# Attention on one core: turned weights weighed four groups at a time, in place of two

## The reference

```
p_c = masked_softmax(q . k_cmp)          # compressed keys, 63 blocks
p_s = masked_softmax(q . k_sel)          # selected blocks: with 1024 tokens, all causal ones
p_w = masked_softmax(q . k_win)          # window of 512
out = gate0 * p_c @ v_cmp + gate1 * p_s @ v_sel + gate2 * p_w @ v_win
```

## Time and profile before

| | |
|---|---|
| time, median of 3 | 1775.0 us (1772.59 to 1776.08) |
| profiled execution | 1776.86 us, its span 1774.8 us |
| TensorE busy | 1667.9 us, 94% of the span |
| VectorE, ScalarE, GpSimd busy | 1134.2, 734.2, 290.0 us |
| granted TensorE clock over the span | 0.966 |
| attention: first turn to last weigh | 392.1 to 653.0 us |

### The profile page before, as it was taken

The page is one execution under the profiler, slowest core; times in us unless marked ns, Lnnn a source line. Parts: engine busy times, 40 slices in busy tenths (PEclk is TensorE's granted clock), DMA queues, the critical chain, the costliest instruction groups (busy, mean ns, idle before and its releaser), DMA issues. The chain is left out here.

```text
span 1774.8 us, 34718 instructions
## 1 busy us (share of the span) xinstructions
PE 1667.9 (94%) x13909; PEld 1534.6 (86%) x13909; DVE 1134.2 (64%) x1886; ACT 734.2 (41%) x1379; POOL 290.0 (16%) x380
## 2 busy tenths in 40 slices
PE   6999999989999979999977897999999989999997
PEld 5999999978888867888753896999999989999997
DVE  6463485238877765766677678878777766545531
ACT  6532332127655554444443433334333344333431
POOL 1000000013333233222121321121121120000000
PEclk8999999999999999999978999999999999999999
DMA  6641265357977326777675761344444487666641
GB/s 183 127 108 36 58 158 166 120 162 229 255 141 139 81 96 229 234 230 243 181 134 166 219 187 59 124 164 138 144 145 165 167 304 248 193 192 185 184 128 54
DMA packets 294030, 287.48 MB, mean 162 GB/s; under 512 B 62238, under 2 KB 248182, under 8 KB 291246
## 3 DMA queue, kind: packets, MB, share of 16 engines
q1 hardware_dynamic: 266398, 179.79, 36.0%
q0 software_dynamic: 25088, 100.94, 18.5%
q10 hardware_dynamic: 2384, 4.53, 1.0%
HBM read 215.36 MB, written 107.60 MB: 182 GB/s over the span
## 5 line engine op out<-in xcount | busy, mean ns | idle before, releaser
L59 PE MATMUL pm<-ops,slots 128*128 128x258 f32 x1792 | 510.1, 285 | 19.7 <-DVE ops L3671 14.7
L60 PE MATMUL pm<-ops,slots 128*128 128x258 f32 x1792 | 508.7, 284 | 0.0
L61 PE MATMUL pm<-ops,slots 128*128 128x258 f32 x1792 | 507.6, 283 | 0.0
L59 PEld LDWEIGHTS pm<-ops,slots 128*128 128x128 f32 x1792 | 339.6, 190 | 20.8 <-DVE ops L3671 15.4
L61 PEld LDWEIGHTS pm<-ops,slots 128*128 128x128 f32 x1792 | 342.1, 191 | 0.0
L60 PEld LDWEIGHTS pm<-ops,slots 128*128 128x128 f32 x1792 | 341.8, 191 | 0.0
L59 PE MATMUL pz<-hH,winH 128*128 128x344 f32 x600 | 199.7, 333 | 1.6 <-DVE hL L845 1.6
L61 PE MATMUL pz<-hH,winL 128*128 128x344 f32 x600 | 193.6, 323 | 0.0
L60 PE MATMUL pz<-hL,winH 128*128 128x344 f32 x600 | 193.5, 323 | 0.0
L3677 DVE TENSOR_TENSOR slots<-uact,slots 128x512 fp32r<-128x512 f32 x160 | 109.6, 699 | 78.8 <-ACT slots L3497 78.5
L3497 ACT ACTIVATE slots<-uact 128x512 fp32r<-128x512 f32 x160 | 99.0, 625 | 126.4 <-DMA uact<-downS_scratch 39.3
(11 more groups left out here) (682 smaller groups left out, 3311.0 us busy)
## 6 DMA issues: line engine op xcount, KB each, us to landing
hidD_scratch<-onat POOLq DMA_DIRECT2D x112, 258.0 KB, 3.0
downS_scratch<-in_w_down_dram POOLq DMA_DIRECT2D x12, 2048.0 KB, 15.7
hs<-hidD_scratch SPq DMA_DIRECT2D x38, 516.0 KB, 4.9
uact<-in_w_up_dram SPq DMA_DIRECT2D x64, 256.0 KB
uact<-downS_scratch SPq DMA_DIRECT2D x64, 256.0 KB, 3.0
raw<-in_w_in_dram SPq DMA_DIRECT2D x24, 512.0 KB, 3.7
uact<-in_w_down_dram SPq DMA_DIRECT2D x48, 256.0 KB, 4.1
wo<-hidD_scratch SPq DMA_DIRECT2D x18, 516.0 KB, 4.7
```

What stands on the lines that cost most here:

```text
L59: nc.tensor.matmul(out, wH, mH, start=start and k == 0, stop=False)
L60: nc.tensor.matmul(out, wH, mL, start=False, stop=False)
L61: last = nc.tensor.matmul(out, wL, mH, start=False, stop=stop and k == n - 1)
```

## The change

The ring of SBUF buffers for turned weights (`ptT`) grows from four to five (`NPT`), the fifth being a tile of its own, `turned_more`, and the order on TensorE becomes: once five turned groups wait, four are weighed (`BATCH`). `craw`, used only at the start of the stage, moves into space that was already set aside. The waits of the copies for their buffer follow the new ring. `pT` stays at two banks, and the placing of the steps does not change. The copy of a finished tile of pO comes one group later in ScalarE's queue.

```diff
+NPT, BATCH = 5, 4
...
-        sb("ahead_rest", [P, 8 * P])
+        ahead_rest = sb("ahead_rest", [P, 8 * P])
...
-        ptT = [free2[:, n * 4 * P:(n + 1) * 4 * P] for n in range(4)]
-        craw = sb("craw", [P, 2, P])
+        turned_more = sb("turned_more", [P, (NPT - 4) * 4 * P])
+        ptT = [free2[:, n * 4 * P:(n + 1) * 4 * P] for n in range(4)] + [turned_more[:, n * 4 * P:(n + 1) * 4 * P] for n in range(NPT - 4)]
+        craw = ahead_rest[:, 0:2 * P].rearrange("p (k c) -> p k c", k=2)
...
-                    bank, src = O[t % 2], ptT[n % 4]
+                    bank, src = O[t % 2], ptT[n % NPT]
...
-                    if len(behind) == 4:
-                        weigh(behind.pop(0))
-                        weigh(behind.pop(0))
+                    if len(behind) == NPT:
+                        for _ in range(BATCH):
+                            weigh(behind.pop(0))
...
-                    if n >= 4:
-                        act.wait_ge(pv_done, n - 3)
+                    if n >= NPT:
+                        act.wait_ge(pv_done, n - NPT + 1)
                     w = len(sched.groups[n][2]) * P
-                    nc.scalar.activation(ptT[n % 4][:, 0:w], PT[n % 2][:, 0:w], ACT.Copy).then_inc(copied_a, 1)
+                    nc.scalar.activation(ptT[n % NPT][:, 0:w], PT[n % 2][:, 0:w], ACT.Copy).then_inc(copied_a, 1)
...
-                    if n - 4 == sched.tile_end[out]:
+                    if out < len(TILE_ORDER) and n - NPT == sched.tile_end[out]:
...
-                    if n >= 4:
-                        dve.wait_ge(pv_done, n - 3)
+                    if n >= NPT:
+                        dve.wait_ge(pv_done, n - NPT + 1)
```

More of the change, by code:

```diff
@@ L1607, in copy_turned @@
                     dve.wait_ge(pt_done, n + 1)
-                    if n >= 4:
-                        dve.wait_ge(pv_done, n - 3)
+                    if n >= NPT:
+                        dve.wait_ge(pv_done, n - NPT + 1)
                     w = len(sched.groups[n][2]) * P
-                    nc.vector.tensor_copy(ptT[n % 4][:, 0:w], PT[n % 2][:, 0:w]).then_inc(copied_v, 1)
+                    nc.vector.tensor_copy(ptT[n % NPT][:, 0:w], PT[n % 2][:, 0:w]).then_inc(copied_v, 1)
                 def gather_rows():
```

## The result

The changed kernel takes 1791.89 us, the median of 5 runs (1788.63 to 1795.98), against 1775.0 us for the one before (now 5 runs, 1772.59 to 1780.2). The ratio is 1.0085, with a 95% interval of 1.0062 to 1.0108: 15 us more, between 11 and 19. It is taken over all runs and is not the quotient of the two medians, which lie 16.9 us apart. The forecast was 1790 us, 15 us more.

What follows compares the result with a forecast made beforehand. TensorE was taken to bound the attention. Between counts of +20 and +5 us, both net of the saving, +15 us was chosen by judgement, giving 1790 us as a median; range 1771 to 1800.

Steps and rivals of the forecast that it cites:

- What the change saves: TensorE's borders between 128- and 64-column matmuls in the attention: 75 visits become 38, saving 11 to 12 us.
- The batches worked through: 15 of 37 attention batches, followed through each engine's queue: sum +8.0 us, mean +0.53 us, net of the saving.
- T17: Attention batch where a turn waits for ScalarE's copy behind exponentials: 7.94 us becomes 8.81 us, losing 0.9 us.
- T125: Attention batch where a turn waits for VectorE's copy: 5.23 us becomes 6.11 us, losing 0.9 us.
- T49: Attention batch where a score waits for pS banks: 0.35 us wait, about the 0.3 us saved, so even.
- The first count: Net loss over the attention's 37 batches, extended from the 15 worked through: +20 us.
- the coarse one: Overruns of attention turns losing their cover, 26.5 us, less old stalls 9.6 and saving 11.8: +5 us.
- Where the waits stand: TensorE waits for copies of turned weights in 40 to 60 places, at T(4m+3) and T(4m+4) alone, 0.3 to 1.7 us each.
- The chain from S29 to T20: Attention, score to turn through ScalarE's exponentials and copy: stays 5.0 to 5.2 us without the weighs between.
- The rival that the borders win: In the attention, idle engines catch up during four weighs, only the saving stays: up to -12 us; faster 0.15.
- The rival of a starved VectorE that then binds: VectorE idles during the attention's four weighs, then binds: +5 us on the 20, 1800 us; chance 0.06.
- The fifth buffer: Extra SBUF buffer for turned weights in the attention: claimed hidden, costed at nothing; otherwise 2 us a batch.

Runs made afterwards that it cites:

- the run of one at a time: One group weighed at a time instead of two, in the kernel before with its four buffers: 1795.43 us, ratio 1.0112.
- the chain cut: Changed kernel with ScalarE's copies of turned weights queued ahead of exponentials and VectorE's ahead of scalings, from group 6 on: 1774.48 us, ratio 0.9997 against the kernel before.

## Why the prediction was right

- *What the change saves*, 37 visits at 0.3 us, 11 to 12 us: the rest fell by 12.4 us, 11.5 without the two groups weighed ahead of T5, and the run of one at a time gives 0.33 us a visit. T20 with its four weighs takes 438.62 - 436.17 = 2.45 us, where 2.46 had been put together from pieces.
- *The batches worked through.* T17 +0.87 us (0.9 forecast), T125 +0.82 (0.9), T49 +0.14 (0), by the starts of the turns in both traces. Of the other twelve, T113 came to -0.29 (-0.3), T121 -0.50 (-0.6), T93 +0.44 (0.4) and T85 +0.92 (0.7); the furthest off are T129, +0.41 for 0.8, and T21, +0.27 for 0.6. All 15 sum to 6.4 us, where 8.0 had been forecast.
- *Which count.* The first count gave +20 us over 37 batches, the coarse one +5, and +15 was chosen between by judgement; no sum gives it, so that the value came out this close is partly luck. The counted stretch shows +15.9. By the starts of the turns all 37 batches, T1 to T149, sum to +17.7 us, a mean of 0.48: 0.43 for the 15 and 0.51 for the other 22. So the 15 were a fair sample, and the first count ran high by 0.1 us for each batch worked. The coarse count had the stalls too small, 26.5 us against 38.5; 7.1 us of the difference of 12.0 are the bank waits that it left out.
- *Where the waits stand.* At T(4m+3) and T(4m+4), as forecast, though not quite alone: 17 and 20 held turns, and T14 and T86. 39 places is just under the 40 to 60 named. The chain from S29 to T20 is 5.03 us, where 5.0 to 5.2 had been forecast.
- *The rival that the borders win* fell because the stalls came to 38.5 us in all, where 21 us, the 9.6 of before and the 11.8 saved, was the point of balance. Its argument, that idle engines would catch up, is what the chain cut refutes: with the same TensorE order and the same work on each engine the loss goes away, and it goes only by moving the copies. Throughput was not what lacked. The rival of a starved VectorE that then binds falls with it: that VectorE is busy for 39.98 of the 50 us from 400 us on, less than the 43.62 of before, shows by itself only that it waits more, but the same work fits once the copies come earlier.
- *The fifth buffer was costed at nothing.* By itself, with two at a time, it costs 2 to 7 us. The reading is that it shifts which turns have a weigh just ahead of them, at the expense of ScalarE's; with four at a time one turn of each engine lacks the weigh in either phase, so it need not add to the 15 us; that is argued, not shown. Against the run with the same ring and two at a time, four at a time has 22.9 us more of stalls and 12.9 us less of rest, 10 us in all, and the ratios are some 10 us apart as well. A ring of four with four at a time was not run. The later copy of a finished tile, also put at nothing, holds one weigh: W6 starts 0.15 us after it ends, 0.2 us late.
- *Not settled.* In the profiled execution the span grew by 11.8 us, but the stage by 18: the part behind it was 6 us shorter. The traces of the other runs put that part between 1115.7 and 1119.9 us, and before at 1121.5 us, so it varies; the medians agree with the stage. Of the 18 us, 2.2 lie ahead of T5: some 0.9 for the two groups more that are weighed there, and the others where the granted clock was at the lower of its two levels (1.2 GHz) for longer, 0.50, 0.50 and 0.57 in the windows 392 to 396, 396 to 400 and 400 to 404 us, against 0.78, 0.50 and 0.86 before. Whether the change has a part in that is open.

The gap at a fixed place that "Perfetto Trace Analysis", section "Optimization Strategy", of the Trainium skill says can mean too few buffers is there, at T(4m+3) and T(4m+4), in front of pT's two banks. Whether a third bank would close it was not tried. What closed most of it, 30.9 us of waits for copies down to 6.3, was two kinds of copies that came earlier, with two banks as before.

## What to carry to other kernels

Work that looks like pure cost on the bounding engine can be the cover of a wait: before batching it, follow what the instructions around it wait for, with the batched work taken out, and compare the chain's length with what is left. When a change of order loses, look at what stands ahead of the late producer in its own queue; moving two kinds of copies ahead of work that was wanted less soon undid 15 us here, and made the kernel before 0.4% faster too. Edits to two engines that feed the same consumer in turn must be judged together, since one alone can move the wait to the other, or to the next reader of the copies.

## What was not expected of the hardware

Leaving the matmuls on 128 columns for those on 64 and coming back costs 0.33 us here, by 73 more such visits in the run of one at a time (24.0 us), and 37 fewer save 11.5 us, 0.31 each. The Trainium skill, "TensorEngine Tiling (Array Packing)", section "Key Properties", says that changing the tiling mode drains TensorE, and the trace agrees; the page gives no figure. Not all of the price need be that. What surprised was that a turn is cheaper in front of a score than in front of another turn: from T17 at 430.78 to S29 at 431.14 are 0.36 us for four pieces, where T128 to T129 took 0.50 us in the trace before and a turn in front of a weigh 0.56 us. So a visit also takes from its turn the cheaper place in front of a score.
